# S5 with every fourth token in a tile: chunks by masked copies and products, phase tables ahead of the tail, rotation in larger steps

## The chip, the cores and the metric

One core of one Trainium2 chip. The time is the device time of one execution in microseconds. The kernel before takes 1168.35 us, the median of 3 runs (1164.45 to 1168.84). Everything is float32.

## The reference

One inference step of a two-layer decoder for 512 prompt tokens and 8 sample tokens (one new token each) with D = 1024. Layer 0 is a pooling mixer beside an mLSTM, then a mixture of experts; layer 1 is an S5 state space with GELU and GLU, then a mixture of experts. The part that the change is about:

```
h = rmsnorm(x, norm_mix[1])                         # (tokens, 1024), 64 groups of 16 channels
lam_bar = exp(lam * dt)                             # 64 complex states per group
h_state[t] = lam_bar * h_state[t-1] + b_bar @ h[t]  # per group; the samples start from their own state
y[t] = real(c @ h_state[t]) + d * h[t]
ag = gelu(y) @ w_glu                                # (1024, 2048)
x = x + ag[:, :1024] * sigmoid(ag[:, 1024:])
x = x + hmoe(rmsnorm(x, norm_ffn[1]))               # top 2 of 8 experts in the best of 4 groups, 32 experts
```

Outputs are y for all tokens and the final states of every part.

## The kernel before

The engines run programs written by hand; semaphores order them, and each DMA queue is the program of the engine that issues it (nearly all are SyncE's). All arrays live in one buffer `arena` [128, ...]; `place(at, ...)` gives a view, so a name stands for an address range and ranges are used again. X holds the tokens as 4 tiles of 128 and one of 8 samples; PSUM is used as a ring of 4 slots of two banks (`PsumRing`, in the order of `jobs_of_kernel`; a job can start when the job four before it has been emptied).

Stages: norm and input projection, mLSTM and pooling, output projection with the router (`router(0, ...)`), experts of layer 0 (`experts(0)`: 16 pairs of experts, their weights through one slot, 6 MB a pair), S5, GLU, `router(1, ...)`, experts of layer 1 (three slots), final norm.

While the experts of layer 0 run, GpSimd builds the S5 matrices (`matrices`): M, which takes a chunk of 8 tokens (8 x 16 channels = 128 rows) to its contribution to the 64 states of a group at the chunk's end, and GR, GI, which take a state to the 8 outputs after it. S5 then goes as follows; the names are those in the code.

- At the end of `experts(0)` VectorE adds the experts' parts to X (L1845, L1850), ScalarE squares and takes roots (L1102, L1112), VectorE scales into H2 (L1860); `h_2` counts the five tiles.
- ScalarE makes two block-diagonal matrices BD (`make_bd`, L1248, L1250), then TensorE forms the taps k = BD x G (L1020, L1021). VectorE copies them to KS, adds the skip term and releases the write to DRAM (`kp`).
- A tile of H2 holds 128 tokens in a row. `regroup` sends each tile by DMA to XK, where partition n holds the 8 tokens of chunk n (16 chunks a tile); two zero blocks come from DRAM (`zr`), and two small transfers put the sample tokens in the last place of 8 extra chunks ahead and in the first place of 8 extra chunks behind. XK has 80 partitions: 8, 64, 8.
- `recut`: for each eighth q of the channels one copy to XR (80 x 1024), eight transposes to PSUM (`u` jobs, L646 in the transposes helper), one copy to U [128, 64 groups, 80]. VectorE and ScalarE take turns.
- TensorE: zs = M x U (L1036), four pairs of groups a q. GpSimd has made the phase tables TC, TS (`phases`, 36 operations at L2034, after `picks_by_pe`), and the samples' decayed states SHR, SHI.
- VectorE, per q: rotates zs into RR, RI (six operations of 128 x 256) and adds the samples' part (two of 128 x 32); then two scans over all chunks (L1937); then, half by half, rotates back into HR, HI (L1423, 128 x 1008); `states_in` releases TensorE at the first half.
- The taps come back from `kp` as TT (L401, eight transfers of 512 KB on the queues of SyncE and ScalarE) once zs 7 is full, since TT lies on M.
- TensorE: y = U x TT + HR x GR + HI x GI per q (L1052, L1056), copied to YK by both engines in turn; then eight transposes per 128 channels (L646) and the GELU on ScalarE to YT (L1387, L1390); then the GLU (L1077).
- SyncE loads the GLU weights over TT and GR when y 3 and y 7 are full, and the first expert weights of layer 1 after that.

## Time and profile before

| | us |
|---|---|
| median of 3 runs | 1168.35 |
| the profiled execution | 1163.01 |
| its span | 1161.1 |
| TensorE matmul busy | 957.9 (82%) |
| TensorE weight load busy | 587.9 (51%) |
| VectorE busy | 426.6 (37%) |
| GpSimd busy | 329.7 (28%) |
| ScalarE busy | 164.9 (14%) |
| mean granted TensorE clock | 0.918 |

In the page of the profile the span is cut in 40 slices of 29 us. TensorE's busy share is 8 or 9 tenths in most of them, and 4 or 5 in the slices around 580 to 725 us; the granted clock falls there too. The share of DMA is at 8 or 9 tenths through both expert stages. The chain of waits is the list of what ended last, each piece followed back from what it released.

### The profile page before, as it was taken

Reading aid. Unit: us, or ns where it says so; the run is one execution under the profiler, and the core shown is the slowest. Engines: PE = TensorE matmul, PEld = TensorE weight load, DVE = VectorE, ACT = ScalarE, POOL = GpSimd, SP = SyncE. Lnnn points to the kernel's source line nnn. Section 1 sums busy time; section 2 is a strip of 40 time slices with the busy share of each in tenths; the row PEclk is TensorE's granted clock in tenths of the full one; section 3 lists DMA queues with packets and bytes.
Section 4 is the critical chain, followed back from the end, with each engine's and each line's share of the span. In section 5 each row is a group of like instructions: output and inputs, shape, how many; then the busy total and the mean of one; then the engine's idle time right before and its main releaser. Section 6 shows DMA issues by size and latency. Waiting matters only on the chain.

```text
span 1161.1 us, 15775 instructions
## 1 busy us (share of the span) xinstructions
PE 957.9 (82%) x5740; PEld 587.9 (51%) x5740; DVE 426.6 (37%) x945; ACT 164.9 (14%) x304; POOL 329.7 (28%) x548
## 2 busy tenths in 40 slices
PE   3999998889698788878864539799996999787776
PEld 2888878545554344434423427444545555443342
DVE  3300065677552222222272891003265423212216
ACT  3201020132200000000041001400433000000002
POOL 0070000187466666565629000000000121111000
PEclk9999989999599999998986659799995899999999
DMA  7126630641679999999957362913008799999975
GB/s 252 37 73 220 220 137 2 238 173 38 270 313 422 423 424 398 402 407 382 371 157 91 45 102 84 389 45 132 32 38 321 292 421 422 425 425 423 422 295 205
DMA packets 53380, 289.37 MB, mean 249 GB/s; under 512 B 11788, under 2 KB 21772, under 8 KB 34600
## 3 DMA queue, kind: packets, MB, share of 16 engines
q1 hardware_dynamic: 38759, 264.69, 58.2%
q0 software_dynamic: 8928, 16.49, 3.8%
q10 hardware_dynamic: 5632, 7.41, 2.9%
q8 instruction: 37, 0.61, 0.2%
q14 instruction: 24, 0.19, 0.1%
HBM read 267.59 MB, written 35.06 MB: 261 GB/s over the span
## 4 chain that ended last, share of the span: by engine, by line
PE 51%; DMA 30%; DVE 9%; SPq 4%; issue 3%; ACT 2%; POOL 1%; DVEq 0%; POOLq 0%; ACTq 0%
DMA arena<-in_w_gu 19%; PE ps L681 12%; PE ps L931 12%; PE ps L808 7%; PE ps L1077 5%; DMA arena<-in_w_down 3%; PE ps L921 3%; DVE arena L1423 3%; DMA arena<-scratch_yd 2%; SPq L515 2%; PE ps L1052 2%; PE ps L1056 2%; DMA arena<-arena 1%; PE ps L838 1%; SPq L444 1%
## 5 line engine op out<-in xcount | busy, mean ns | idle before, releaser
L931 PE MATMUL ps<-arena 128*64 128x256 f32 x2048 | 245.6, 396 | 67.1 <-DMA arena<-in_w_gu 65.6
L931 PEld LDWEIGHTS ps<-arena 128*64 128x64 f32 x2048 | 150.2, 142 | 164.2 <-DMA arena<-in_w_gu 57.4
L2100 POOL TENSOR_TENSOR arena<-arena 128x256 f32<-128x256 f32 (+3 forms) x192 | 132.1, 688 | 40.7 <-POOL arena L2100 40.3
L681 PE MATMUL ps<-arena 128*128 128x260 f32 x640 | 141.4, 383 | 0.0
L681 PEld LDWEIGHTS ps<-arena 128*128 128x128 f32 x640 | 121.1, 190 | 18.8 <-issue 0.4
L921 PE MATMUL ps<-arena 128*64 128x512 f32 x512 | 118.8, 606 | 13.4 <-DMA arena<-in_w_down 12.9
L2034 POOL TENSOR_TENSOR arena<-arena 128x32 f32<-128x32 f32 (+5 forms) x165 | 82.8, 502 | 156.8 <-ACTq L1237 141.3
L1792 DVE TENSOR_TENSOR arena<-arena,ps 128x128 f32<-128x128 f32 x64 | 18.4, 288 | 276.5 <-ACT arena L1326 276.5
L808 PE MATMUL ps<-arena 128*128 128x512 f32 x256 | 115.8, 603 | 2.5 <-DVE arena L1569 2.4
L1326 ACT ACTIVATE arena<-ps 128x128 f32<-128x128 f32 x64 | 17.7, 277 | 493.9 <-PE ps L931 493.9
L2131 POOL COPY idx_now<-idx_list 128x1 int32 (+1 forms) x32 | 6.1, 192 | 274.4 <-DVEq L1707 249.0
L808 PEld LDWEIGHTS ps<-arena 128*128 128x128 f32 x256 | 47.6, 192 | 57.9 <-issue 54.2
L921 PEld LDWEIGHTS ps<-arena 128*64 128x64 f32 x512 | 36.0, 138 | 74.4 <-issue 62.6
L1814 DVE TENSOR_TENSOR arena<-ps,arena 128x512 f32<-128x512 f32 x60 | 41.5, 692 | 70.5 <-PE ps L921 70.5
L1423 DVE TENSOR_TENSOR arena<-arena 128x32 f32<-128x32 f32 (+17 forms) x110 | 59.4, 540 | 14.7 <-PE ps L669 7.3
L646 PE MATMUL ps<-arena 128*128 128x128 f32 (+6 forms) x234 | 31.5, 304 | 36.8 <-DVE arena L1135 16.1
L1077 PE MATMUL ps<-arena 128*128 128x512 f32 x128 | 58.1, 618 | 4.4 <-ACT arena L1390 4.4
L2143 POOL COPY idx_now<-idx_dest 128x1 int32 (+1 forms) x30 | 5.4, 181 | 179.4 <-DVE arena L1814 179.2
L646 PEld LDWEIGHTS ps<-arena 128*128 128x128 f32 (+6 forms) x234 | 27.4, 178 | 41.4 <-issue 22.3
L1052 PE MATMUL ps<-arena 128*72 128x128 f32 x128 | 22.2, 299 | 27.9 <-DVEq L1948 27.9
L1077 PEld LDWEIGHTS ps<-arena 128*128 128x128 f32 x128 | 25.3, 199 | 36.5 <-issue 32.0
L1784 DVE TENSOR_TENSOR arena<-ps,arena 128x512 f32<-128x512 f32 x64 | 41.1, 682 | 4.4 <-PE ps L901 4.4
(220 smaller groups left out, 987.1 us busy)
## 6 DMA issues: line engine op xcount, KB each, us to landing
arena<-in_w_gu SPq DMA_DIRECT2D x64, 2048.0 KB, 13.1
arena<-in_w_down SPq DMA_DIRECT2D x64, 1024.0 KB, 14.2
arena<-in_w_in SPq DMA_DIRECT2D x10, 1024.0 KB, 6.1
scratch_yd<-arena SPq DMA_DIRECT2D x2, 4160.0 KB, 16.4
arena<-scratch_yd SPq DMA_DIRECT2D x16, 512.0 KB, 7.8
arena<-in_w_out SPq DMA_DIRECT2D x1, 4096.0 KB, 12.7
scratch_hd<-arena ACTq DMA_DIRECT2D x8, 512.0 KB
arena<-in_w_glu SPq DMA_DIRECT2D x2, 2048.0 KB, 7.8
```

The lines of the kernel that those rows point to most:

```text
L646: mm = pe.transpose(out, in_, ident[0:k, 0:k])
L681: mm = pe.matmul(o[:, b, 0:HALF], w[:, kc, (n % 2) * P:(n % 2 + 1) * P], HT[:, kc, b * HALF:(b + 1) * HALF], start=kc == 0, stop=kc == KC - 1)
L808: mm = pe.matmul(o[:, b, :], x[:, kc, i * P:(i + 1) * P], w[:, kc, b * 512:(b + 1) * 512], start=kc == 0, stop=kc == KC - 1)
L921: mm = pe.matmul(ps[CAP * s:CAP * s + CAP, 6 + b, :], AT[l][s][:, CAP * f:CAP * f + CAP], WD[l][i][b][:, 2 * s + f], start=f == 0, stop=f ...
L931: mm = pe.matmul(ps[CAP * f:CAP * f + CAP, 2 + s, 0:256], XT[l][:, kc, CAP * s:CAP * s + CAP], WGU[l][i][s][:, kc, 256 * f:256 * f + 256], ...
L1052: pe.matmul(outs[b], U[:, 2 * pr + b, NS:UC], TT[:, 2 * pr + b], start=True, stop=False)
L1077: mm = pe.matmul(o[0:n, b, :], YT[:, kc, i * P:i * P + n], WGL[0][:, kc, b * 512:(b + 1) * 512], start=kc == 0, stop=kc == KC - 1)
L1423: step(v.tensor_tensor(out, a, b, op))
L1784: v.tensor_tensor(XT[l][:, 4 * b:4 * b + 4], ps[:, b, :].rearrange("p (k t) -> p k t", k=4), spread(GK[:, l, 4 * b:4 * b + 4], P), ALU.mul ...
L1814: v.tensor_tensor(YE[l][half][:, 512 * b:512 * b + 512], ps[:, 6 + b, :], w, ALU.mult).then_inc(sem(f"y_ready_{l}"), 1)
L2034: step(g_.tensor_tensor(out, a, b, op))
L2100: g_.tensor_tensor(o, x, y, f).then_inc(sem("matrix_steps"), 1)
```

## The change

What it does, part by part:

- **Order of tokens.** From the output projection of layer 0 on, tile i holds the tokens i, i + 4, i + 8, ... The projection reads its columns at that step (`MIX[:, kc, i:SEQ:TILES]`), X is loaded again from the input in that order (four transfers, waited for by the first addition), the output is written back in that order, and the GELU writes YT so.
- **Chunks.** XK, `regroup`, `zr` and their transfers are gone. A chunk of 8 tokens is then two neighbouring partitions, m = 2k and 2k + 1, of the four tiles. `recut` writes XR [128 x 1024] with two masked copies (a multiplication by a 0/1 column `parity`), so that each partition fills only its half of the 8 places, and XS [40 x 1024] with two small copies of the samples. Each transpose becomes two products: XR with `couple` [128 x 64], which adds the two partitions of a chunk, and XS with `pick` [40 x 16].
- **Block-diagonal copies.** `make_bd` is called after the root of tiles 0 and 1 in `experts(0)`. The scratch of the squares is H2 itself.
- **Taps.** ScalarE copies KS, GpSimd adds the skip term after the phase tables. TT comes in two halves of 8 transfers of 256 KB, the first when zs 3 is full, the second when zs 7 is.
- **Phase tables.** GpSimd waits for `down_done_0` (and `xt_done_0`), not for the last pick.
- **Rotation.** Per q two operations of 128 x 512 from PSUM, a copy of the samples' columns, and two of 128 x 256; four q's, two scans over half the pairs, rotation back of that half in six operations of 128 x 1008 and six small ones for the end states; then the second half.
- **Tail of S5.** ScalarE copies y 0 to 3, VectorE y 4 to 7; the transposes of q - 2 follow the columns of q, and the GELUs run beside them.
- **Places and loads.** YT and several buffers of layer 1 are moved; the down weights of slot 2 in layer 1 are loaded after the router's last logits.

The diff, cut to its core:

```diff
@@ -83,6 +86,12 @@
+    put("couple", (p[:, None] // 2 == np.arange(NCH)[None, :]).astype(np.float32))
+    m = np.zeros((XSROWS, 2 * NS), np.float32)
+    m[np.arange(NS), np.arange(NS)] = 1.0
+    m[XSROWS - NS + np.arange(NS), NS + np.arange(NS)] = 1.0
+    put("pick", m)
+    put("parity", (p[:, None] % 2 == np.arange(2)[None, :]).astype(np.float32))
...
@@ -392,14 +405,15 @@
-def regroup(eng, i):
-    n = NS + i * P // L
-    eng.dma_start(XK[n:n + P // L], H2[:, i, :]).then_inc(sem("xk_in"), 16)
-def taps(eng, s):
+def taps(eng, s, half):
-    eng.dma_start(TT[CW * s:CW * s + CW], kg[:, :, KZERO - CW * s:KZERO - CW * s + P]
-                  ).then_inc(sem("taps_in"), 16)
+    gs = slice(GU // 2 * half, GU // 2 * half + GU // 2)
+    eng.dma_start(TT[CW * s:CW * s + CW, gs], kg[:, gs, KZERO - CW * s:KZERO - CW * s + P]
+                  ).then_inc(sem(f"taps_in_{half}"), 16)
+def every_fourth(x, i):
+    return x.rearrange("(m i) d -> i m d", i=TILES)[i]
...
@@ -476,6 +488,8 @@
+    for i in range(TILES):
+        load(X[:, i, :], every_fourth(T["x_prompt"], i), "x_again")
...
@@ -579,30 +593,21 @@
-    sp.wait_ge(sem("kz_out"), 64)
-    sp.wait_ge(sem("h_2"), 1)
-    load(XK[0:NS, 0:L - 1].rearrange("p l d -> p (l d)"), zr[0:NS], "xk_in")
-    load(XK[NS + NCH:UC, 1:L].rearrange("p l d -> p (l d)"), zr[NS:2 * NS], "xk_in")
-    sp.wait_ge(sem("x_moe"), 1)
+    sp.wait_ge(sem("kz_out"), 48)
+    sp.wait_ge(sem("v_ready"), EP)
-    for i in range(0, TILES, 2):
-        sp.wait_ge(sem("h_2"), i + 1)
-        regroup(sp, i)
-    sp.wait_ge(sem("h_2"), 5)
-    load(XK[0:NS, L - 1, :], H2[0:NS, TILES], "xk_in")
-    load(XK[NS + NCH:UC, 0, :], H2[0:NS, TILES], "xk_in")
-    ring.wait_full(sp, "zs", 7)
-    for s in range(L // 2):
-        taps(sp, s)
-    sp.wait_ge(sem("states_in"), 3)
+    for half in range(2):
+        ring.wait_full(sp, "zs", 4 * half + 3)
+        for s in range(L // 2):
+            taps(sp, s, half)
+    sp.wait_ge(sem("states_in"), 4)
-    sp.wait_ge(sem("taps_in"), 16 * L)
...
@@ -619,16 +624,18 @@
+    sp.wait_ge(sem("routed"), routed(1, "lg", 4))
-    sp.wait_ge(sem("routed"), routed(1, "lg", 4))
...
@@ -805,7 +812,7 @@
-                    mm = pe.matmul(o[:, b, :], x[:, kc, i * P:(i + 1) * P], w[:, kc, b * 512:(b + 1) * 512],
+                    mm = pe.matmul(o[:, b, :], tokens_of(kc, i), w[:, kc, b * 512:(b + 1) * 512],
...
@@ -1022,9 +1031,14 @@
+        ring.wait_free(pe, "u", q)
-        transposes(("u", q), [(o[:, j // 4, (j % 4) * UC:(j % 4 + 1) * UC],
-                               XR[q % 2][:, j * P:(j + 1) * P]) for j in range(8)])
+        for j in range(8):
+            out = o[:, j // 4, (j % 4) * UC:(j % 4 + 1) * UC]
+            pe.matmul(out[:, NS:SC], XR[q % 2][:, j * P:(j + 1) * P], const("couple"), start=True, stop=True)
+            ends = out.rearrange("p (a b) -> p a b", b=NS)[:, 0:UC // NS:UC // NS - 1]
+            mm = pe.matmul(ends, XS[q % 2][:, j * P:(j + 1) * P], const("pick", XSROWS), start=True, stop=True)
+        full(mm)
...
@@ -1037,13 +1051,13 @@
-    pe.wait_ge(sem("taps_in"), 16 * L)
-    pe.wait_ge(sem("states_in"), 1)
-    for q in range(8):
+    def columns(q):
-        if q == 4:
-            pe.wait_ge(sem("states_in"), 2)
+        if q % 4 == 0:
+            pe.wait_ge(sem(f"taps_in_{q // 4}"), 16 * L)
+            pe.wait_ge(sem("states_in"), 3 if q else 1)
...
@@ -1055,11 +1069,19 @@
-    for kc in range(KC):
+    def turned(kc):
+        at = (kc % 4) * P
+    for q in range(8):
+        columns(q)
+        if q >= 2:
+            turned(q - 2)
+    for kc in (6, 7):
+        turned(kc)
...
@@ -1136,18 +1158,25 @@
-def recut(eng, step, copy, odd):
+def recut(eng, step, copy, masked, copy_zeros, odd):
+    copy_zeros(XS[odd])
+    eng.wait_ge(sem("h_2"), 5)
-        copy(XR[odd].rearrange("p (g l c) -> p l g c", g=8, l=L),
-             XK[:, :, q * P:(q + 1) * P].rearrange("p l (g c) -> p l g c", c=CW)
-             ).then_inc(sem(f"xr_ready_{odd}"), 1)
+        xr, xs = (b[odd].rearrange("p (g l c) -> p l g c", g=8, l=L) for b in (XR, XS))
+        for s in range(2):
+            step(masked(xr[:, 4 * s:4 * s + 4],
+                        H2[:, 0:TILES, q * P:(q + 1) * P].rearrange("p i (g c) -> p i g c", c=CW),
+                        const("parity")[:, s:s + 1]))
+        sample = H2[0:NS, TILES, q * P:(q + 1) * P].rearrange("p (g c) -> p g c", c=CW)
+        step(copy(xs[0:NS, L - 1], sample))
+        copy(xs[XSROWS - NS:XSROWS, 0], sample).then_inc(sem(f"xr_ready_{odd}"), 1)
...
@@ -1338,11 +1374,13 @@
-        junk = JUNK[l]
+        junk = [place(A + 38048, D)] * 5 if l else [H2[:, t, :] for t in range(5)]
-            tile_squares(act, 2 * l + 2, t, junk)
+            tile_squares(act, 2 * l + 2, t, junk[t])
+            if l == 0 and t < 2:
+                make_bd(t, step)
...
@@ -1351,43 +1389,62 @@
-    for q in range(2):
-        make_bd(q)
-        act.wait_ge(sem("h_2"), 2 * q + 2)
-        regroup(act, 2 * q + 1)
-    act.wait_ge(sem("xk_in"), 128)
-    ring.wait_full(act, "k")
-    recut(act, step, a.copy, 1)
+    take(act, "k")
+    give(act, a.copy(KS.rearrange("p a b -> p (a b)"), slot_flat("k")), "k")
+    act.sem_inc(sem("ks_ready"), 1)
+    zeros = before[:, 0:1]
+    def zero(out):
+        step(a.copy(out, zeros[0:XSROWS].broadcast_to((XSROWS, D))))
+    recut(act, step, a.copy, lambda out, x, m: a.activation(out, x, ACT.Copy, scale=m), zero, 1)
+    act.wait_ge(sem("phases_ready"), 1)
+    step(a.copy(R8, spread(mag8, NCH)))
+    a.copy(R8[:, :, 0:1], zeros.unsqueeze(1).broadcast_to((P, PAIRS, 1))).then_inc(sem("ks_ready"), 1)
-    ring.wait_full(act, "zs", 7)
-    for s in range(L // 2, L):
-        taps(act, s)
-    act.wait_ge(sem("states_in"), 3)
+    for half in range(2):
+        ring.wait_full(act, "zs", 4 * half + 3)
+        for s in range(L // 2, L):
+            taps(act, s, half)
-    for q in range(1, 8, 2):
-        y_out(q)
-    for kc in range(KC):
+    def gelu(kc):
-        if kc == 0:
-            ring.wait_full(act, "y", 7)
-        step(a.activation(YT[:, kc, 0:SEQ].rearrange("p (k b l) -> p b l k", b=2, l=4),
+        if kc == 3:
+            act.wait_ge(sem("states_in"), 2)
+        step(a.activation(YT[:, kc, 0:SEQ].rearrange("p (i k s) -> p s i k", i=4, s=2),
+    for q in range(4):
+        y_out(q)
+        if q >= 2:
+            gelu(q - 2)
+    for kc in range(2, KC):
+        gelu(kc)
...
@@ -1636,6 +1693,8 @@
+        if k == 0:
+            dve.wait_ge(sem("x_again"), 16 * TILES)
...
@@ -1898,61 +1957,78 @@
...
+    recut(dve, step, v.tensor_copy, lambda out, x, m: v.tensor_scalar(out, x, m, None, ALU.mult),
+          lambda out: step(v.memset(out, 0.0)), 0)
+    def rotated(q):
+        half, at = q // 4, 4 * (q % 4)
+        chunks = z[:, :, :, NS:SC]
+        out = RRI[half][:, :, at:at + 4]
+        tt(out, chunks, spread_mid(TC[half][:, at:at + 4], 2), ALU.mult)
+        tt(TMQ, chunks, spread_mid(TS[half][:, at:at + 4], 2), ALU.mult)
+        give(dve, v.tensor_copy(SZ[:, :, 4 * q:4 * q + 4], z[:, :, :, 0:NS]), "zs", q)
+        tt(out[:, 0], out[:, 0], TMQ[:, 1], ALU.add)
+        tt(out[:, 1], out[:, 1], TMQ[:, 0], ALU.subtract)
+    def scanned(half):
+        decay = R8[:, PAIRS // 2 * half:PAIRS // 2 * (half + 1)].rearrange("p r k -> p (r k)")
+        for ri in range(2):
+            f = RRI[half][:, ri].rearrange("p r k -> p (r k)")
+            step(v.tensor_tensor_scan(f, decay, f, 0.0, ALU.mult, ALU.add))
+    def states(half):
+        for end, a_, b_, op in ((ends[0], x, y, ALU.subtract), (ends[1], y, x, ALU.add)):
+            tt(end, a_[:, :, n], tc[:, :, n], ALU.mult)
+            tt(last, b_[:, :, n], ts_[:, :, n], ALU.mult)
+            tt(end, end, last, op)
+        for o, h0 in ((hr, H0R), (hi, H0I)):
+            step(v.tensor_copy(o[:, :, NCH:SC], h0.rearrange("p (r n) -> p r n", n=NS)[:, prs]))
+        tt(hr[:, :, 1:NCH], x[:, :, 0:n], tc[:, :, 0:n], ALU.mult)
+        tt(hi[:, :, 1:NCH], y[:, :, 0:n], tc[:, :, 0:n], ALU.mult)
+        tt(x[:, :, 0:n], x[:, :, 0:n], ts_[:, :, 0:n], ALU.mult)
+        tt(y[:, :, 0:n], y[:, :, 0:n], ts_[:, :, 0:n], ALU.mult)
+        tt(hr[:, :, 1:NCH], hr[:, :, 1:NCH], y[:, :, 0:n], ALU.subtract)
+        tt(hi[:, :, 1:NCH], hi[:, :, 1:NCH], x[:, :, 0:n], ALU.add)
+    for q in range(4):
+        rotated(q)
+    dve.wait_ge(sem("ks_ready"), 2)
+    scanned(0)
+    dve.wait_ge(sem("s5_in"), 160)
+    states(0)
+    for q in range(4, 8):
+        rotated(q)
+    scanned(1)
+    dve.sem_inc(sem("states_in"), 1)
+    states(1)
+    dve.sem_inc(sem("states_in"), 1)
+    dve.wait_ge(sem("phases_ready"), 2)
+    for ri, o in enumerate((SHR, SHI)):
+        tt(o, o, SZ[:, ri], ALU.add)
+    dve.sem_inc(sem("states_in"), 1)
+    for q in range(4, 8):
...
@@ -2197,12 +2273,17 @@
-    pool.wait_ge(sem("picks_by_pe"), 6)
-    step(g_.memset(TC[:, :, 0:1], 1.0))
-    step(g_.memset(TS[:, :, 0:1], 0.0))
+    pool.wait_ge(sem("xt_done_0"), E + 4)
+    pool.wait_ge(sem("down_done_0"), E)
+    step(g_.memset(TURNS[:, :, 1, :, 0:1], 1.0))
+    step(g_.memset(TURNS[:, :, 0, :, 0:1], 0.0))
+    tt(SKIP, spread_mid(const("diag"), KC), spread(DSK, CW), ALU.mult)
+    pool.wait_ge(sem("ks_ready"), 1)
+    tt(KS[:, :, 0:CW], KS[:, :, 0:CW], SKIP, ALU.add)
+    pool.sem_inc(sem("taps_ready"), 1)
```

## Rows read from the trace of the kernel before

**Rows 1.** Chain of waits, 600 to 760: start us, us, what
```profile
605.08 1.30 DVE arena L1860
...
613.75 16.11 DMA arena<-arena
...
641.77 2.14 PE ps L1036 x32
...
686.94 1.10 PE ps L1052 x4
...
740.46 19.88 PE ps L1077 x39
```

**Rows 2.** Timeline of SyncE's queue: start us, us, issue
```profile
157.51 0.33 SPq L444 DMA_DIRECT2D arena<-in_c  x1
```

**Rows 3.** Page, groups: busy, mean ns of one, idle before and its cause
```profile
L808 PEld LDWEIGHTS ps<-arena 128*128 128x128 f32 x256 | 47.6, 192 | 57.9 <-issue 54.2
```

**Rows 4.** Timeline of VectorE and ScalarE at the end of the layer-0 experts
```profile
596.70 0.15 DVE L1107 TENSOR_SCALAR arena<-arena 128x1 f32<-128x1 f32 x1
...
604.60 1.04 ACT L1248 COPY arena<-arena 128x1024 f32<-128x1024 f32 x1 [0.78 <-issue]
...
605.68 1.27 ACT L1250 COPY arena<-arena 64x512 f32<-64x512 f32 x2
```

**Rows 5.** Timeline of GpSimd and TensorE, 600 to 694: start us, us
```profile
600.98 35.24 POOL L2034 TENSOR_TENSOR arena<-arena 128x32 f32<-128x32 f32 x36
...
609.45 0.68 PE L1020 MATMUL ps<-arena 128*32 128x128 f32 x8 [8.97 <-ACT arena L1250]
...
615.20 0.34 PE L1020 MATMUL ps<-arena 128*32 128x128 f32 x4 [2.12 <-issue]
...
636.82 2.40 PE L646 MATMUL ps<-arena 80*128 80x80 f32 x16 [0.24 <-DVE arena L1148]
...
692.58 0.66 PE L1052 MATMUL ps<-arena 128*72 128x128 f32 x4
693.17 0.66 PE L1056 MATMUL ps<-arena 64*72 64x128 f32 x8
```

**Rows 6.** Timeline of TensorE: three runs of short products behind whole-width loads
```profile
59.53 0.96 PE L691 MATMUL ps<-arena 120*128 120x8 f32 x8
...
280.91 1.87 PE L838 MATMUL ps<-arena 128*128 128x36 f32 x16
...
877.66 3.60 PE L838 MATMUL ps<-arena 128*128 128x36 f32 x16 [0.84 <-ACT arena L1269]
```

**Rows 7.** Stretches: length; busy us of PE, PEld, DVE, ACT, POOL; clock; DMA; GB/s
```profile
149.00:152.40 3.40, 3.40 (x5) 1.33 (x4) 1.66 (x4) 1.59 (x6) 0.00 (x0) 0.50 0.54 218
299.00:303.00 4.00, 4.00 (x19) 3.94 (x19) 2.81 (x14) 1.24 (x1) 0.44 (x2) 0.50 0.99 349
...
613.20:620.00 6.80, 2.41 (x75) 2.14 (x75) 2.28 (x3) 0.00 (x0) 6.25 (x8) 1.00 1.10 129
631.70:641.70 10.00, 9.59 (x65) 8.65 (x65) 6.26 (x7) 4.90 (x6) 8.95 (x8) 0.50 0.01 2
...
660.60:684.20 23.60, 0.00 (x0) 0.00 (x0) 22.40 (x33) 0.00 (x0) 0.00 (x0) 0.50 1.19 176
898.00:908.00 10.00, 8.82 (x46) 5.56 (x48) 5.34 (x17) 0.28 (x1) 1.21 (x2) 0.56 0.10 26
...
740.40:746.30 5.90, 5.84 (x7) 2.52 (x8) 0.00 (x0) 0.00 (x0) 0.00 (x0) 0.50 1.01 433
```

**Rows 8.** Groups of VectorE by form, 641.8 to 697: busy, mean ns, idle
```profile
L1423 DVE TENSOR_TENSOR arena<-arena 128x1008 f32<-128x1008 f32 x12 | 14.5, 1208 | 0.4
L1423 DVE TENSOR_TENSOR arena<-ps,arena 128x256 f32<-128x256 f32 x32 | 13.6, 425 | 1.8 <-PE ps L1036 0.8
L1937 DVE TENSOR_TENSOR_SCAN arena<-arena 128x2048 f32<-128x2048 f32 x2 | 8.8, 4424 | 0.1
...
L1957 DVE COPY arena<-ps 72x512 f32<-72x512 f32 x1 | 0.7, 686 | 0.2 <-DVE arena L1423 0.2
```

**Rows 9.** Groups of ScalarE by form, 604 to 742
```profile
L1387 ACT ACTIVATE arena<-ps 128x512 f32<-128x512 f32 x8 | 8.8, 1098 | 0.2
```

More of the change, by code:

```diff
@@ L31 @@
 SC = NCH + NS
+XSROWS = 32 + NS
 E = 32
@@ L47 @@
                   ("iota", P), ("reve", E), ("revg", 4), ("tokid", 10),
-                  ("row", 10), ("ramp", 4 * CW), ("head", 4 * P), ("last", P), ("diag", CW)]:
+                  ("row", 10), ("ramp", 4 * CW), ("head", 4 * P), ("last", P), ("diag", CW),
+                  ("couple", NCH), ("pick", 2 * NS),
+                  ("parity", 2)]:
     CONST[_name] = (_at, _n)
@@ L314, in bass_hybrid_step @@
         WD = [[[place(A + 8192 + 2048 * b, 4, 512) for b in range(2)]],
[L315 removed]
+              [[place(A + at + 2048 * b, 4, 512) for b in range(2)] for at in (0, 20480, 16384)]]
         XG = [[place(A + at + D * b, D) for b in range(2)] for at in (12288, 4096)]
@@ L1900, in experts @@
                 dve.sem_inc(sem("x_tile"), 5)
-                dve.sem_inc(sem("x_moe"), 1)
             router(0, mixed)
             experts(0)
-            take(dve, "k")
-            give(dve, v.tensor_copy(KS.rearrange("p a b -> p (a b)"), slot_flat("k")), "k")
-            tt(SKIP, spread_mid(const("diag"), KC), spread(DSK, CW), ALU.mult)
-            tt(KS[:, :, 0:CW], KS[:, :, 0:CW], SKIP, ALU.add)
-            dve.sem_inc(sem("taps_ready"), 1)
-            dve.wait_ge(sem("xk_in"), 128)
@@ new lines, in _ @@
+            n = NCH - 1
+            def states(half):
+                prs = slice(PAIRS // 2 * half, PAIRS // 2 * (half + 1))
+                x, y = RRI[half][:, 0], RRI[half][:, 1]
+                tc, ts_ = TC[half], TS[half]
+                hr, hi = HR[:, prs], HI[:, prs]
+                ends = [HEND[:, q, prs] for q in range(2)]
+                last = TMQ[:, 0, 0, 0:PAIRS // 2]
+                for end, a_, b_, op in ((ends[0], x, y, ALU.subtract), (ends[1], y, x, ALU.add)):
[3 more added lines that the diff above has]
+                for o, h0 in ((hr, H0R), (hi, H0I)):
+                    step(v.memset(o[:, :, 0:1], 0.0))
+                    step(v.tensor_copy(o[:, :, NCH:SC], h0.rearrange("p (r n) -> p r n", n=NS)[:, prs]))
[5 more added lines that the diff above has]
+                tt(hi[:, :, 1:NCH], hi[:, :, 1:NCH], x[:, :, 0:n], ALU.add)
```

133 lines of the change are left out of this document (59 added, 74 removed).

## The prediction

> **What bounds the kernel now.** I read the chain of waits first. In layer 1 TensorE and the weight stream set the end, and the change leaves both as they are, so I looked for the stretch in which neither works. It lies between the last row of the layer-0 normalisation, which ends at 606.38 us (605.08 + 1.30), and the first GLU product at 740.46 [rows 1]: 134.1 us in which TensorE is idle or short of work. The reader is to see four parts there. From 606.38 to 629.89 everything waits for the four regrouping transfers (the 16.11 us piece, DMA arena<-arena). To 641.77 the pieces are transposed. To 686.94 VectorE rotates, scans and rotates back. Then come the column products to 726.8 and eight GELUs, one after the other, to 740.1. All that comes later follows the GLU, so the difference of the program is the shift of that 740.46.
>
> The profiled execution took 1163.01 us (span 1161.1), the three timed runs 1168.35 at the median; I sum against 1163.0 and add the same 5.3 us at the end.
>
> **Ahead of the S5 stage.** The constants grow by 82 columns on 1448 (41 KB on 724 KB); the x rows behind them come about 0.2 us later, and they begin the chain. The four reloads of x are issued at about 145.6, behind the load of the norms; SyncE's next load goes out at 157.5 [rows 2], and they are needed at 246: hidden; without that cover the next load would slip by 4 issues of about 0.5 us. The projection's weights are now read at every fourth column. A weight load there takes 0.19 us of the 0.43 us between two products of 512 columns, 0.24 is free, mostly put down to issue [rows 3]: nothing, unless the stride more than doubles it; at double and a half again, 128 loads would cost some 6 us.
>
> The block-diagonal copies move from behind the normalisation into its ScalarE chain. Each is 1.04 + 2 x 0.62 = 2.35 us with its gaps [rows 4]. The first sits between the root of tile 0 and the squares of tile 1, which VectorE waits for. Squares 1 then end at about 598.3, not 595.7; VectorE's variance 1 was issued behind an addition until 596.7, so 1.7 us of the 2.5 show; the second block adds as much again. I follow it to the last row: 609.8, not 606.4, **+3.4**. In exchange TensorE can begin the tap products (k) as soon as the last addition is in (605.3 and about 1 us of branch) at 606.4, not at 609.45. They took 8.1 us, 609.45 to 617.6, 2.1 of it a stall [rows 5]; so they end at 614.5. VectorE's first masked block (branch 0.8, zero fill about 0.9, two products of 512 at 0.6, two copies of 0.2) is ready at 613.1, just ahead of that.
>
> **The chunks by products.** Before, forming U took 64 transposes, 16 in 2.4 us [rows 5]. Now each of 64 pieces takes two ordinary products (64 columns from all 128 rows, 16 columns from 40 rows). The trace shows an ordinary float32 product as two records, a transpose as one: 64 x 2 x 2 = **256 records**, each with a weight load of 128 columns. The price of such a record does not hang on its few moving columns: at full clock L838, 36 columns, takes 1.87 us for 16 with the 0.2 that the last runs on, 0.107 each, and L691, 8 columns, 0.96 us for 8, 0.10 to 0.13 each; at half clock L838 takes 3.60 us, 0.213 each [rows 6]. So the stage costs 256 x 0.107 = 27.4 us at full clock, 54.6 at half. VectorE and ScalarE need only some 2.5 us for a q each (2 x 0.6, 2 x 0.2, 0.8 for the copy out), against 6.8 for two q's on TensorE even at full clock: they no longer set it.
>
> Which clock? The rows say half. In 299 to 303 TensorE is busy the whole time with just such short products behind whole-width loads, and is granted 0.50; 149 to 152.4 is at 0.50 although it had been busy without a pause (products of 4 rows since 145.4); the transposes of 631.7 to 641.7 stay at 0.50 too [rows 7]. After the tap products the clock was at 1.00 from 613.2 to 620 [rows 7] and then fell. I take that once more: 5.5 us of the stage at full clock (51 records for 26), the rest at half, 54.6 - 5.5 = 49.1, and 0.4 for hand-overs: the stage ends at **664.0**, where before it ended at 641.8: **+22.2**.
>
> The Trainium skill (TensorE: Matmul & The Clock Gate, on LDWEIGHTS) says that a weight load takes its number of columns divided by 1.2 GHz, whatever the rows. By that the loads would cost 107 ns at either clock, the stage 27.3 us, and the end would be that of the first rival below; L838's two rates [rows 6] speak against the one price, and the measurement decides.
>
> **Rotation, scan, rotation back.** Say T0 is the time at which the first zs block is full: 2.2 us after the end of U, as 641.8 to 644.0 before. Per q VectorE did 6 operations of 256 and 2 of 32 in 3.20 us. Now two of 512 from PSUM (0.69, spaced 0.72), a copy (0.22) and two of 256 (0.43, spaced 0.46): 2.58 [rows 8]. Four q's 10.3, two scans of 1024 at half of 4.43 each 4.5, then six small operations 1.5, fills and copies 0.8, six of 1008 at 1.24 7.4: y can start at T0 + 24.5, where it took 42.9. The second half costs the same again: T0 + 49.1.
>
> Taps: 4 MB took 23.6 us (660.6 to 684.2 at a DMA share of 1.19) [rows 7]. Half of it, issued when zs 3 is full (T0 + 6.6), lands by about T0 + 20.5, 4 us ahead of the states; the second half by T0 + 33. The write of the taps waits for the phase tables, which start on GpSimd at about 583.3 instead of 600.5, take the same 35.2 us [rows 5], and end at 618.8; written by 630. Hidden.
>
> Columns: y0 6.8 us from a half-clock start, then 4.72 each (eight groups, 0.59 from start to start [rows 5]). With two blocks of eight transposes, 0.56 each, between, the first four end at T0 + 24.5 + 22.1 = T0 + 46.6 and wait 2.5 us for the states of the second half: T0 + 49.1. Four more and four turned ones: 21.1, T0 + 70.2. Then the copy of y7 (1.4), its transposes and the last GELUs (1.10 and 0.18 each [rows 9], the first five now hidden beside the columns): GLU at **T0 + 74.5**, where it was 644.0 + 96.4. That is **-21.9**.
>
> **Sum.** T0 = 664.0 + 2.2 = 666.2; GLU at 740.7, where it was 740.46: +0.2 (22.2 - 21.9). The constants +0.2. The GLU began at half clock (0.50 to 746 [rows 7]) after 14 us of little work; now 5 us after the last columns, so I give it 1.5 of the up to 3 us. The clock may fall in the 2.5 us pause: +1. Layer 1: one pair of down loads waits for the last logits, 8 us later; the DMA share is 0.10 from 898 to 908 and the loads before it only just drain [rows 7], so nothing. The 2 MB of the GLU's second half come 5 us ahead of its start and are needed 7 us into it: nothing. Total about 0 to +1: **1164** against the profile, **1169** against the median.
>
> Bounds of what the trace doesn't show. Clock in the U stage: all half (+5.5) or all full (-21.7). A 40-row load between 128-row ones: the cheapest row is the rate of L691 and L838 (0 extra), the dearest L1052, four records of 128 moving columns in the 0.59 us to the next group, 0.147 each [rows 5], where L741 takes 0.11 with 129: 0.037 more at full clock, 0.074 at half, on 51 and 205 records +17. I take 0, as L691 (120 rows, 8 columns) is nearest. Masked copies: between 0.43 and 1.25 us each, hidden either way. Tap halves: 12 us, or as long as the whole, 24.
>
> **The rivals.**
> *The clock holds.* If the U stage stays at full clock it ends at 614.5 + 27.4 = 641.9, T0 = 643.2, GLU at 717.7: -22.8, with 2 for the GLU's start -25: 1138, **1144** at the median. For it: TensorE is busy without a pause. Against: three stretches of [rows 7]. 0.15. The skill's rule of thumb on the same page (why this matters for your kernels) would have it: keep TensorE continuously busy and it stays at its full rate. The 299 to 303 row does not bear it out.
> *Alternating row heights spoil the overlap of loads and products.* Price 0.074 us a record at half clock, place the U stage, +17: 1180, **1186**. It decides against the change from 0.03 us a record on. For it: L1052 and L1056, which alternate whole and half height, pay 0.147 for 128 columns where L741 pays 0.11 for 129. Against: L1052 pays it also within its own four. 0.20.
> *The tap halves are no shorter than the whole* (the price per transfer, not per byte): y starts at T0 + 32.2, its second half at T0 + 54.3, +5: **1174**. 0.13. For it: four issues took 8.55 us on one queue. Against: share 1.19, the engines were the limit.
> My own case, 0.52, holds 1160 to 1178.
>
> **How the numbers follow.** 0.5% (5.8 us) is about what a measurement of this kernel tells from no change. Faster: the first rival 0.15 and 0.13 of mine. Slower: the second 0.20, 0.07 of the third, 0.09 of mine. Same: the rest. Eight in ten: 1148 to 1186.
>
> **What would show it.** U products: 256 records, PE busy without a gap for about 50 us at 0.50; a stage of 27 us would make the forecast wrong by the first rival, one of 65 by the second. The last normalised row at about 609.8. VectorE 2.6 us a q. y start 24.5 us after the first zs; a wait for the transfer of the taps there would be the third. GLU 74.5 us after the first zs.

## The result and the profile after

The changed kernel takes **1201.0 us**, the median of 4 runs (1194.1 to 1204.6); the kernel before, beside it, 1168.6 (4 runs, 1164.5 to 1168.8). The ratio is **1.0288**, with 95% interval 1.0256 to 1.0320: slower by 32 us. The forecast was 1169, its range 1148 to 1186, and the measured time lies outside it. What happened is the second rival (17 us forecast, 19 measured), and on top of it 7 us ahead of the S5 stage that no rival had.

The profiled execution took 1194.1 us, span 1192.3 (before 1163.0, 1161.1), a difference of 31.2. All of it is there when the GLU begins: its first product starts at 771.24, where it was 740.46 [rows 1], +30.8. From there to the end it is 421.1 us after and 420.6 before. First the page of the kernel after, two groups with the number of records, busy us and mean ns, idle before:

```profile
L815 PEld LDWEIGHTS ps<-arena 128*128 128x128 f32 x256 | 62.4, 251 | 48.4 <-issue 33.0
...
L1038 PE MATMUL ps<-arena 128*128 128x64 f32 x128 | 42.6, 435 | 0.5 <-DVE arena L1179 0.5
```

L1038 is the product of the chunks; with L1040, that of the samples, these are the forecast's 256 records. L815 answers to L808 of [rows 3]: the mean load has gone from 192 to 251 ns. The stretches of the kernel after that answer to [rows 7] (length; busy us and records of PE, PEld, DVE, ACT, POOL; granted clock; DMA share; GB/s):

```profile
623.40:627.00 3.60, 3.60 (x22) 3.13 (x22) 0.00 (x0) 3.35 (x6) 3.52 (x2) 0.99 0.00 0
627.00:694.00 67.00, 67.00 (x234) 57.99 (x233) 12.36 (x16) 8.48 (x16) 13.74 (x13) 0.50 0.03 8
771.20:777.00 5.80, 5.76 (x7) 2.52 (x8) 0.00 (x0) 0.00 (x0) 0.00 (x0) 0.50 1.08 460
```

In the second row PE is busy for 67.0 of 67 us at the half clock, as forecast, but for 67 us, where the forecast had 205 x 0.213 = 44. TensorE waits for nobody; the weight loads fill only 58 of the 67. The timeline shows the records in pairs (start, length; a length runs into the next), first at the full, then at the half clock, and below them where the tail begins:

```profile
623.37 0.43 PE L1038 MATMUL ps<-arena 128*128 128x64 f32 x2 [0.50 <-DVE arena L1179]
623.73 0.39 PE L1040 MATMUL ps<-arena 40*128 40x16 f32 x2
624.05 0.43 PE L1038 MATMUL ps<-arena 128*128 128x64 f32 x2
...
649.77 0.69 PE L1038 MATMUL ps<-arena 128*128 128x64 f32 x2
650.39 0.61 PE L1040 MATMUL ps<-arena 40*128 40x16 f32 x2
650.92 0.69 PE L1038 MATMUL ps<-arena 128*128 128x64 f32 x2
...
697.08 1.42 DVE L1480 TENSOR_TENSOR arena<-ps,arena 128x512 f32<-128x512 f32 x2 [10.56 <-PE ps L1050]
...
723.44 0.22 DVE L1979 COPY arena<-ps 128x64 f32<-128x64 f32 x1
...
723.72 1.13 PE L1066 MATMUL ps<-arena 128*72 128x128 f32 x4 [15.78 <-DVE arena L1979]
...
771.24 4.61 PE L1099 MATMUL ps<-arena 128*128 128x512 f32 x5 [1.39 <-ACT arena L1440]
```

From one L1038 to the next, four records, it is 0.68 us at the full clock and 1.15 at the half: 0.171 and 0.288 a record, where the forecast had 0.107 and 0.213. The start of the U stage, in the chain of waits of the kernel after (start us, us, what):

```profile
614.30 1.67 DVE arena L1919
...
617.85 0.92 DVE arena L1966
618.79 0.92 DVE arena L1965
619.74 1.17 DVE arena L1965
620.93 0.98 DVE arena L1178
621.94 1.38 DVE arena L1179
623.32 0.04 issue
623.37 0.43 PE ps L1038 x2
```

The last normalised row ends at 616.0, the first masked block with its samples is complete only 7.3 us later; 3.3 were forecast.

### The profile page after: what moved, and what is told of

Same layout as the page of the kernel before. It is cut to its first block, busy times and chain, and to the rows that moved or that the text cites. A ratio compares the mean times of both kernels' runs of the same rounds, so it can differ in the third digit from the quotient of the medians.

```text
span 1192.3 us, 16177 instructions
## 1 busy us (share of the span) xinstructions
PE 1025.3 (86%) x5932; PEld 655.4 (55%) x5932; DVE 431.6 (36%) x939; ACT 169.9 (14%) x320; POOL 333.8 (28%) x550
## 4 chain that ended last, share of the span: by engine, by line
PE 54%; DMA 29%; DVE 7%; SPq 4%; issue 2%; ACT 2%; POOL 1%; DVEq 0%; POOLq 0%; ACTq 0%
DMA arena<-in_w_gu 19%; PE ps L688 12%; PE ps L938 10%; PE ps L815 8%; PE ps L1099 5%; DMA arena<-in_w_down 4%; PE ps L1038 3%; PE ps L1040 3%; PE ps L928 2%; SPq L529 2%; DMA arena<-scratch_yd 2%; DVE arena L1480 2%; PE ps L1070 2%; PE ps L1066 2%; PE ps L845 1%
## 5 line engine op out<-in xcount | busy, mean ns | idle before, releaser
L938 PE MATMUL ps<-arena 128*64 128x256 f32 x2048 | 248.3, 398 | 64.6 <-DMA arena<-in_w_gu 62.7
L2110 POOL TENSOR_TENSOR arena<-arena 128x32 f32<-128x32 f32 (+5 forms) x167 | 90.5, 542 | 161.8 <-ACTq L1273 146.1
L688 PEld LDWEIGHTS ps<-arena 128*128 128x128 f32 x640 | 121.5, 191 | 20.0 <-issue 0.4
L815 PE MATMUL ps<-arena 128*128 128x512 f32 x256 | 119.8, 620 | 2.5 <-DVE arena L1626 2.4
L815 PEld LDWEIGHTS ps<-arena 128*128 128x128 f32 x256 | 62.4, 251 | 48.4 <-issue 33.0
L1099 PE MATMUL ps<-arena 128*128 128x512 f32 x128 | 58.2, 617 | 1.4 <-ACT arena L1440 1.4
L1099 PEld LDWEIGHTS ps<-arena 128*128 128x128 f32 x128 | 25.2, 198 | 33.7 <-issue 32.2
L1038 PE MATMUL ps<-arena 128*128 128x64 f32 x128 | 42.6, 435 | 0.5 <-DVE arena L1179 0.5
L908 PE MATMUL ps<-arena 128*128 128x128 f32 x256 | 39.9, 282 | 3.3 <-DMA arena<-scratch_hd,idx_now 3.3
L2210 POOL DMA_INDIRECT arena<-scratch_hd,idx_now x32 | 34.1, 1065 | 27.6 <-POOL idx_now L2207 22.4
```

Of the source, the lines that this page charges most:

```text
L688: mm = pe.matmul(o[:, b, 0:HALF], w[:, kc, (n % 2) * P:(n % 2 + 1) * P], HT[:, kc, b * HALF:(b + 1) * HALF], start=kc == 0, stop=kc == KC - 1)
L815: mm = pe.matmul(o[:, b, :], tokens_of(kc, i), w[:, kc, b * 512:(b + 1) * 512], start=kc == 0, stop=kc == KC - 1)
L908: mm = pe.transpose(ps[:, b, q * P:(q + 1) * P], XG[l][half][:, kc * P:(kc + 1) * P], ident)
L938: mm = pe.matmul(ps[CAP * f:CAP * f + CAP, 2 + s, 0:256], XT[l][:, kc, CAP * s:CAP * s + CAP], WGU[l][i][s][:, kc, 256 * f:256 * f + 256], ...
L1038: pe.matmul(out[:, NS:SC], XR[q % 2][:, j * P:(j + 1) * P], const("couple"), start=True, stop=True)
L1099: mm = pe.matmul(o[0:n, b, :], YT[:, kc, i * P:i * P + n], WGL[0][:, kc, b * 512:(b + 1) * 512], start=kc == 0, stop=kc == KC - 1)
```

## The experiments

Each is the changed kernel with one edit, unless another base is named. The ratio is always to the kernel before, from runs on the same chip. The first starts of the stages in the profiled executions, in us, are used throughout (U: first product or transpose of the chunks; zs: first product behind them):

```
                       projection  experts     k      U     zs    GLU    span
before                      217.8    316.8  609.5  631.7  641.7  740.5  1161.1
after                       222.2    324.0  617.4  623.4  694.8  771.2  1192.3
e1_grouped                  223.8    325.3  621.5  632.9  689.9  766.4  1184.9
e2_full_height              222.1    321.9  616.1  626.3  681.0  757.6  1177.3
e3_no_pick                  220.6    322.3  618.7  629.1  659.1  735.6  1156.0
e4_contiguous               220.5    319.3  611.3  618.8  690.0  766.7  1186.2
e5_transposed               220.4    320.7  616.7  625.4  643.6  721.7  1141.6
e6_no_reload                220.5    321.8  616.1  623.9  696.3  772.8  1195.2
e7_phases_late              221.9    322.9  614.7  621.1  691.0  767.5  1188.1
e8_not_interleaved          222.4    324.2  617.7  625.4  697.9  778.5  1199.5
e9_samples_by_act           220.4    322.2  613.9  619.8  633.2  710.3  1133.1
e10_mix_in_order            221.8    321.0  617.7  623.2  637.2  714.2  1136.4
e11_columns_mirrored        223.7    326.3  622.5  628.2  642.7  719.0  1140.8
```

### The order of the row heights

```
                for j in range(8):
-                   pe.matmul(chunks j); pe.matmul(samples j)
+                   pe.matmul(chunks j)
+               for j in range(8):
+                   pe.matmul(samples j)
```

> The same 128 fp32 products of the U stage, but in each group of eight first the eight of 128 rows, then the eight of 40 rows, so the row height changes 2 times in 32 records and not 16 times. The stage took 71.4 us in the changed kernel (0.28 us a record). Theory A (a change of row height between neighbouring loads spoils the overlap of load and product): the stage falls towards 256 x 0.213 = 55 us, the program from 1201 to about 1185. Theory B (each record of such a dense row of short fp32 products pays for its load and its product one behind the other, whatever the heights): the stage stays at 70 to 72 us, the program at 1199 to 1203.

Measured: 1184.1 us (1179.3 to 1190.2), ratio 1.0133 [1.0074, 1.0193]. The stage takes 57.0 us for 71.4.

```
-   m = np.zeros((XSROWS, 2 * NS)); XS of XSROWS rows; const("pick", XSROWS)
+   m = np.zeros((P, 2 * NS));      XS of 128 rows;    const("pick")
```

> The samples' blocks and the matrix that picks them are 128 rows high (88 of them zeros), so all 256 records have one height. Theory A: stage 55 us, program about 1185. Theory B: 71 us or slightly more, program 1200 to 1204.

Measured: 1179.9 us (1174.4 to 1183.4), ratio 1.0109 [1.0079, 1.0138]. The stage takes 54.7 us. A stretch inside the stage, first of e1, then of e2 (columns as above):

```profile
633.00:686.00 53.00, 53.00 (x239) 51.91 (x240) 8.67 (x16) 8.23 (x15) 10.90 (x11) 0.50 0.03 11
```

```profile
627.00:680.00 53.00, 53.00 (x251) 53.00 (x250) 9.32 (x16) 8.24 (x15) 12.76 (x12) 0.50 0.04 11
```

The reader is to look at PEld. With one height throughout, the loads stand back to back, 53.0 of 53 us, and 54.7 / 256 = 0.214 us a record is exactly the forecast's price. In the changed kernel they left 9 of 67 us open. Theory A holds and B falls: the same 256 records, with rows of zeros added, are 17 us shorter. The clock is no rival here: all three have 0.50 in these stretches. The runs agree on a price. e1 keeps 16 changes of height and lies 57.0 - 54.7 = 2.3 us over e2, 0.14 us a change. In the changed kernel four records with two changes take 1.15 us at the half clock, where four of e2 take 4 x 0.214 = 0.86: 0.15 a change, and for its 128 changes 19.2 us. 54.7 + 19.2, less the 2.4 us that its 20 records at the full clock saved, is 71.5; 71.4 was measured.

```
-                   mm = pe.matmul(samples j)
```

> Leaves out the 64 products that bring the samples' rows (the samples' outputs are not computed from their inputs). 128 records of 128 rows are left. Theory A: 128 x 0.213 = 27 us for the stage, program about 1201 - 44 = 1157. Theory B: each record of this line keeps its 0.31 us: 128 x 0.31 = 40 us, less the first 3 us at the full clock, so 37 to 40 us, program about 1168. In both the stage is still bound by TensorE; if VectorE and ScalarE (masked copies and evictions) bound it, the profile would show TensorE waiting.

Measured: 1157.5 us (1153.6 to 1160.3), ratio 0.9904 [0.9874, 0.9934]; the samples' products are left out. The stage takes 30.0 us, 43.5 us fall away from the program. Theory A's number for the program was right, for the stage it was 3 us short: in it TensorE now waits about 2 us for VectorE.

### The strided weights and the reload

```
-   router(0, MIX, lambda kc, i: MIX[:, kc, i:SEQ:TILES], ...)
+   router(0, MIX, lambda kc, i: MIX[:, kc, i * P:(i + 1) * P], ...)
```

> The first projection reads its weights at neighbouring columns again, the rest as in the changed kernel (so tokens meet the wrong residual). In the changed kernel the projection took 76.5 us from first to last product and 73.7 before, and the start of the experts stood 7.2 us later. Theory C (the stride costs what the projection itself shows): 2 to 3 us back, program about 1198; the other 4.4 us, which are there before the projection begins, stay. Theory D (all 7 us hang on the stride): program about 1194. Theory E (the stride is hidden): nothing, 1201.

Measured: 1196.4 us (1188.0 to 1198.0), ratio 1.0249 [1.0208, 1.0289]. The loads of the first projection (shortest / median / longest ns, first and last start), in the kernel after and in e4:

```profile
L815 PEld LDWEIGHTS ps<-arena x128: 307/308/337, 222.2 to 298.3; 128*128 128x128 f32 x128
```

```profile
L815 PEld LDWEIGHTS ps<-arena x128: 186/189/337, 220.4 to 294.5; 128*128 128x128 f32 x128
```

Every fourth column makes a load 1.6 times as long, at the full clock. Most of the 128 x 0.12 = 15 us is hidden behind the products, as forecast. From first to last product the projection takes 76.5 us in the kernel after and 74.5 here, 73.7 in before, and 76.5 to 77.1 in nine of the ten kernels that stride. But the tenth, e2, takes 74.7, and the granted clock is not the same. The stretch of the projection in before, after, e2 and e4 (columns as above):

```profile
217.81:291.55 73.74, 70.79 (x266) 35.38 (x266) 53.48 (x98) 17.94 (x28) 51.85 (x134) 0.98 0.29 109
222.21:298.74 76.53, 74.86 (x265) 50.24 (x266) 54.00 (x100) 17.95 (x28) 53.14 (x141) 0.94 0.29 105
222.06:296.73 74.67, 72.88 (x265) 50.11 (x266) 53.85 (x99) 17.95 (x28) 52.66 (x136) 0.97 0.30 108
220.46:294.92 74.46, 72.41 (x265) 35.77 (x266) 53.54 (x98) 17.95 (x28) 52.40 (x133) 0.96 0.30 108
```

The nine slower ones were granted 0.94 to 0.95. So the projection is 2 to 3 us longer, but a good part of that is a lower clock; e2, which strides at 0.97, is only 0.2 us above e4. Whether the stride brings the clock down is not shown. The interval of the time takes in all three theories, C, D and E.

```
-   for i in range(TILES): load(X[:, i, :], every_fourth(T["x_prompt"], i), "x_again")
```

> Leaves out the second load of the prompt (2 MB, beside the mLSTM), so the residual has the wrong token order. In the profile after, the projection starts 4.4 us later than before (222.2 for 217.8), and the reload is the only thing that the change adds ahead of it. Theory G (the reload delays the loads or the steps of the mLSTM): projection at about 218, program 3 to 5 us below the changed kernel (1197). Theory H (the shift is TensorE's clock, which falls at other places from run to run): program within 1 us of 1201 in the median, starts of the projection scattered over the runs.

Measured: 1199.1 us (1195.1 to 1204.6), ratio 1.0280 [1.0235, 1.0326]; it leaves out the reload. The projection starts at 220.5, among the 220.4 to 223.8 of the kernels that reload. The reload is hidden, as forecast. What remains is that all twelve profiles with the change start it 2.6 to 6 us later than the single profile of before. That this one profile, at 1163.0 the shortest execution of before, is the odd one would explain it. Against that: the profile of the kernel after is the shortest of its runs too, and the medians lie 32 us apart where the profiles lie 31. The cause of this shift was not settled.

### The copies beside GpSimd, and the order in the tail

```
    pool.wait_ge(sem("down_done_0"), E)
+   pool.wait_ge(sem("h_2"), 5)
    ... phase tables
```

> GpSimd begins the phase tables only when the fifth normalised tile is there (616 us in place of 596.6). Theory I (GpSimd beside VectorE slows the small copies and the last normalised tile): the last tile takes 1.28 us again and not 1.66, h_2 comes 0.4 us sooner; but the first sample copies still run beside the phases (0.97 and 1.37 us, 0.22 without). The tables end at about 655, still ahead of the first rotation (697): program 0 to 1 us lower. Rival J (GpSimd is late for the taps, whose skip term it adds after the tables): taps written at 658, read at 701: no effect either. The branch stall of TensorE before the k taps (9.8 us) stays in both.

A single execution: 1190.0 us, which tells nothing beside the 1194 to 1205 of the kernel after. VectorE from the last normalised row on, with GpSimd starting at 614.4 (start, us, engine, line):

```profile
612.97 1.29 DVE L1919 SCALAR_TENSOR_TENSOR arena<-arena 128x1024 f32<-128x1024 f32 x1
616.16 0.91 DVE L1966 MEMSET arena<- 40x1024 f32 x1 [1.90 <-issue]
617.10 1.04 DVE L1965 TENSOR_SCALAR arena<-arena 128x512 f32<-128x512 f32 x2
618.18 0.25 DVE L1178 COPY arena<-arena 8x128 f32<-8x128 f32 x1
618.47 0.35 DVE L1179 COPY arena<-arena 8x128 f32<-8x128 f32 x1
```

In the kernel after the same rows take 1.66, 0.91, 2.11, 0.97 and 1.37 us. So the masked block needs 2.7 us from its clearing on, not 5.5. Theory I expected the gain on the last row and missed the larger one on the copies: they now stand beside GpSimd's first steps of 32 and 64 columns, not beside its 512-column ones. On the path it is worth 0.5 us in the kernel after, the wait between the last k product and the first one of the chunks (the row 623.37); in e1, e2 and e3 the same block comes 4.7 to 5.6 us after the last k product. Rival J's end is right as well: the tables end at 653.5, still ahead of the rotation.

```
-   per q: columns(q), turned(q - 2)
+   columns(0..7), then turned(0..7)
```

> All eight y products first, then all eight transposes with their GELUs, as before the change; all else as in the changed kernel. Theory K (interleaving takes six groups of transposes out of the end of the tail): the GLU starts 6 groups x about 1.1 us = 6 to 7 us later, program about 1207. Theory L (the tail is bound by VectorE's second half and its last y evictions, so that transposes behind it are beside waits anyway): 2 to 3 us, program 1203.

Measured: 1200.9 us (1198.2 to 1203.1), ratio 1.0283 [1.0251, 1.0316], no change in time that these runs resolve. In the profile the first rotation to the GLU takes 78.3 us (700.25 to 778.54) for 74.2, so 4 us, between the two theories. The interval of the time (4 us either side) can't tell 4 us from nothing.

### A version that is faster than both

The U stage is worth 71 us at most. In the next kernel a group of eight is formed by 4 transposes of 128x128 and 4 of the samples' 8 rows, 64 in all:

```
    out = o[:, 0, a * P:(a + 1) * P]                       # bank 0: 4 x (two groups x (tile, channel)), tokens m
    pe.transpose(out, XR[q % 2][:, a * P:(a + 1) * P], ident)
    pe.transpose(o[:, 1, a * NS:(a + 1) * NS], XS[q % 2][:, a * P:(a + 1) * P], ident[0:NS, 0:NS])
    # the eviction picks m even into partitions 0:64, m odd into 64:128, for each parity b of the group:
    copy(U[64 * s:64 * s + 64, 8 * q + b:8 * q + 8:2, NS:SC], o[64 * b:64 * b + 64, 0, ..., s::2])
```

> The chunks of S5 are formed without products: per group of eight, 4 transposes of 128x128 (from a plain copy in the order channel group, tile, channel) and 4 of the samples' 8 rows, 64 transposes in all where there were 128 fp32 products; the evictions pick even and odd rows of a tile (strides of 2, half the partitions each). From the transposes of the same shape before the change (64 in 10 us, 0.156 us each, and the less for 8 rows) TensorE has about 8 us of work. Theory A or B (the U stage is bound by its 256 records): TensorE leaves the path, the stage falls from 71 us to what VectorE and ScalarE take for 4 groups each: a copy of 0.65 us, a clearing and two samples' copies of 0.2 us, eight evictions, about 3 us a group on ScalarE, so 13 to 18 us. Program 1201 - 55 = 1146, range 1142 to 1152: faster than the kernel before the change. Theory F (the copies beside a busy GpSimd are the hidden second bound, or the phases, which end at 636 us, and the kernel's response from DRAM come late): stage 25 to 30 us, program 1155 to 1160.

Measured: **1146.8 us** (1143.7 to 1151.7), ratio 0.9836 [0.9803, 0.9870]. The time is theory A's to a microsecond. The stage takes 18.2 us, at the upper end of the 13 to 18, and begins 2.4 us after the last k product, so from there to the first zs product it is 20.6. VectorE, ScalarE and GpSimd in e5:

```profile
621.26 12.99 POOL L2121 TENSOR_TENSOR arena<-arena 128x1024 f32<-128x1024 f32 x6
...
621.49 1.82 DVE L1186 COPY arena<-arena 8x128 f32<-8x128 f32 x1
623.35 1.96 DVE L1187 COPY arena<-arena 8x128 f32<-8x128 f32 x1
...
625.91 0.30 ACT L1186 COPY arena<-arena 8x128 f32<-8x128 f32 x1
...
640.15 0.22 DVE L1187 COPY arena<-arena 8x128 f32<-8x128 f32 x1
```

The same copy of 8x128 takes VectorE 1.96 us while GpSimd works on 1024 columns, and 0.22 when GpSimd is done (at 640.0). One of GpSimd's six operations takes 1.9 to 2.4 us, and they end at 623.23 and 625.23; VectorE's two copies end at 623.31 and 625.31, each 0.08 us behind. ScalarE takes 0.30 beside it. That VectorE waits for the whole of an operation of GpSimd is what the Trainium skill states (SBUF — State Buffer, Who interferes with whom): copies and tensor_scalar may take a port pair that the two engines share, and whoever issues first holds it for the whole instruction. The trace agrees, and e9 uses it; its base is e5:

```
+   act: clear XS once; wait h_2 == 5; 4 copies of 8 rows x 512 (all samples of all q)   # while it waits for k
-   both engines, per q: 2 copies of 8x128 and a clearing of U's ends
+   act: one clearing of U's ends
```

> As the transposed version, but ScalarE builds all the samples' blocks (two clearings and four copies, while it waits for the k taps) and clears U's ends; VectorE keeps one plain copy a group and its evictions. In the transposed version the U stage took 21 us (622.6 to 643.6), and VectorE's 16-partition-short copies of 8x128 took 1.8 to 2.0 us each while GpSimd worked beside it (0.22 to 0.36 after GpSimd was done); ScalarE's took 0.30 throughout. Theory M (VectorE beside GpSimd is what holds the stage): the stage falls to 13 to 15 us, program from 1146.8 to 1140. Rival N (another wait takes its place, the phase tables that end at 634 or the evictions): stage 18 to 20 us, program 1144 to 1146.

Measured: **1137.1 us** (1135.0 to 1140.9), ratio **0.9752** [0.9728, 0.9776], the fastest here and 29 us below the kernel before. From the last k product (619.9) to zs (633.2) it is 13.3 us for 20.6, theory M's number. The operations taken from VectorE would be 4 x 0.6 = 2.4 us at the price they have without GpSimd, so most of the 7.3 us is the waiting:

```profile
620.00:633.20 13.20, 10.62 (x66) 8.14 (x65) 10.49 (x29) 10.97 (x30) 12.73 (x7) 0.68 0.01 2
```

Two further edits of e9. One writes MIX in the order in which the projection reads it:

```
-   give(act, activation(MIX[:, g] ..., slot("pw", g)[:, :, 0:HALF]))
+   three pieces into MIX[:, g, 0:SEQ].rearrange("p (i m) -> p m i", i=TILES), and the samples
-   MIX[:, H:2 * H, c * P:(c + 1) * P]
+   MIX[:, H:2 * H, 0:SEQ].rearrange("p h (i c m) -> p h c m i", i=TILES, c=TILES)[:, :, c]
```

> As e9, and MIX is written in the order in which the first projection reads it (VectorE's and ScalarE's writes ahead of it go out at a stride of 128 columns, ScalarE in three pieces for one), so the 128 weight loads are contiguous again. Theory C (the stride costs 2 to 3 us of the projection): 2 to 3 us below e9, about 1137. Rival O (the strided writes and ScalarE's 8 further pieces of about 0.3 us stand on the path ahead of the projection and eat it): equal to e9 within 1 us.

Measured: 1139.5 us (1137.9 to 1142.2), ratio 0.9770 [0.9748, 0.9792]: nearest to rival O, 2.4 us above e9 at the median, which the intervals can't tell from nothing. The projection is shorter (74.5 for 76.8 us), but it starts 1.4 us later.

```
    j even: the four records of 128 rows, then the eight of 64 rows
+   j odd:  the eight of 64 rows, then the four of 128 rows
```

> Base is e9. In the column products each pair takes four records of 128 rows and then eight of 64 rows, 0.59 us each at the full clock, eight changes of height per q. Here every second pair takes its products in mirrored order, so that neighbours of one height meet and four changes per q are left. Theory P (any change of height between neighbouring loads costs what 128 to 40 rows cost, 19 us / 128 changes = 0.15 us at half clock, 0.13 at full): a q falls from 4.72 to about 4.2 us, the second half of y, which is on the path, is 2 us shorter, program about 1135 (e9: 1137). Theory Q (128 and 64 rows do not pay, or other records bound the q): 4.72 us a q as before, program 1137.

Measured: 1141.0 us (1136.6 to 1142.7), ratio 0.9762 [0.9735, 0.9789]: not told from e9. The rate is theory P's. One q of e9 and of e11, with the transposes (L653) that follow it:

```profile
696.65 0.60 PE L1068 MATMUL ps<-arena 128*72 128x128 f32 x4
697.19 0.66 PE L1072 MATMUL ps<-arena 64*72 64x128 f32 x8
697.78 0.66 PE L1068 MATMUL ps<-arena 128*72 128x128 f32 x4
698.37 0.66 PE L1072 MATMUL ps<-arena 64*72 64x128 f32 x8
698.96 0.66 PE L1068 MATMUL ps<-arena 128*72 128x128 f32 x4
699.55 0.66 PE L1072 MATMUL ps<-arena 64*72 64x128 f32 x8
...
701.33 0.72 PE L653 MATMUL ps<-arena 72*128 72x72 f32 x8
```

```profile
706.49 0.60 PE L1070 MATMUL ps<-arena 128*72 128x128 f32 x4
707.02 1.10 PE L1078 MATMUL ps<-arena 64*72 64x128 f32 x16
708.05 1.10 PE L1070 MATMUL ps<-arena 128*72 128x128 f32 x8
709.08 1.10 PE L1078 MATMUL ps<-arena 64*72 64x128 f32 x16
710.11 0.66 PE L1070 MATMUL ps<-arena 128*72 128x128 f32 x4
710.61 0.67 PE L653 MATMUL ps<-arena 72*128 72x72 f32 x8
```

4.68 us a q become 4.12. The cleanest piece is 24 records inside a q: from 697.19 to 699.55 in e9 they have four changes of height and take 2.36 us, from 707.02 to 709.08 in e11 two changes and 2.06 us. That is 0.15 us a change, at the full clock and between 128 and 64 rows. One row limits the rule. In e11 the last four records of 128 rows stand before transposes of 72 rows (710.11 to 710.61), and there they take 0.50 us and not 0.59: from 128 to 72 rows no price is seen. What all this should save on the path, under 2 us, is below the scatter of the time; from the first zs product to the GLU it is 76.3 us for 77.2.

## Why the prediction was wrong

**The step that failed** is in "Bounds of what the trace doesn't show": "A 40-row load between 128-row ones: ... I take 0, as L691 (120 rows, 8 columns) is nearest." It wasn't: L691's loads all have one height, so it could say nothing of a change of height. The row that could was L1052 beside L1056 [rows 5], which alternates 128 and 64 rows, and which the forecast used only for the dear end. Measured: 0.15 us a change, 19.2 us in all, where the rival had 17. e2 shows that it is the height, since nothing else of those products changed, and e1 that it is the change and not the 40 rows themselves. e11 shows that L1052's price was the same thing. The forecast's argument against ("L1052 pays it also within its own four") misread the timeline, which puts a group of four in one row. Narrow windows on the trace of before, at the half clock, part them:

```profile
689.31 0.85 PE L1052 MATMUL ps<-arena 128*72 128x128 f32 x3
689.74 0.42 PE L1052 MATMUL ps<-arena 128*72 128x128 f32 x1
690.09 0.49 PE L1056 MATMUL ps<-arena 64*72 64x128 f32 x2
```

The first row holds two steps to the last L1052, 0.21 us each, and from there to the first L1056 it is 0.35. At the full clock, from 693 on, it is 0.11 inside a group and 0.20 at its end. So the price could be read before the change was run. The Trainium skill has a rule for this that the forecast didn't weigh: changing the tiling mode, not just the tile, drains TensorE (TensorEngine Tiling (Array Packing), Key Properties). The measured 0.15 us agree with it; that the drain is the mechanism, no run here shows.

**The U stage otherwise.** Half clock from 626.8 on: right. The full clock lasted 3.4 us of it and not 5.5, for 20 records and not 51; these 31 records cost 31 x 0.107 = 3.3 us more. A record at one height costs 0.213 at half clock (e2: 0.214): right, and so the first rival fell by the clock alone. VectorE and ScalarE don't set the stage: right in the changed kernel.

**Ahead of it.** This is the second term that failed: the sum had next to nothing there. The last row was forecast at 609.8 and came at 616.0, 9.6 us later than before. Of these 9.6, 7.1 had come about upstream (the experts started 7.2 us later) and 2.5 in the normalisation itself, where 3.4 were forecast for the block-diagonal copies. Of the 7, 2.8 are in the projection, where "nothing, unless the stride more than doubles it" stood: the load grew to 1.6 times, and the granted clock was 0.94 for 0.98. How the 2.8 divide between the two is open (e4, e2). The other 4.4 are there when the projection starts; they are not the reload (e6), and their cause is open.

**The k taps** were forecast to start 1 us after the last addition. They started 6.2 after it (611.17 to 617.39), 4.8 in e7 and e9. The profile names no wait there; the code has the branch of the experts' loop, and that this branch takes the time was not tested apart. It cost nothing here, since the first block came later still (623.3). VectorE's own branch took 1.9, not 0.8, and its copies 4.5, not 1.6, beside GpSimd; so the stage started 1.8 us later than 614.5 + 7.1.

**The phase tables** began at 596.6, not at 583.3, took 39.2 us and not 35.2, and ended at 636: hidden, but with 17 us less to spare, and in the way of VectorE.

**The tail** was right. Rotation 2.64 us a q (2.58 forecast), GLU 74.2 us after T0, the first rotation (74.5), so 22 us gained. Inside it two errors cancel. y started at T0 + 26.6, not 24.5: not for the taps (the third rival; their first half had landed at 717.1, T0 + 20.0, where 20.5 was forecast), but because y0 uses the PSUM buffer of zs 4, which VectorE empties only behind the states of the first half (the row 723.44 above, and PE's 723.72). The GELUs took 0.64 us and not 1.10. The GLU began at the half clock again (the stretch from 771.2, 0.50), so the 1.5 us that I gave it did not come.

**The sum again**, from the parts: T0 was forecast at 666.2 and is 697.1. That is 7.1 from upstream, 1.8 at the start of U, 71.4 - 49.5 = 21.9 in the stage, 0.1 behind it: 30.9. The tail then keeps its -22.
